# Two RWKV-style layers and an attention block: features turned inside weight blocks, preparation without GpSimd's arithmetic and barrier, recurrence calls joined through the next call's keys

## What is computed

```python
p = h @ w_in                       # gates, u, v of the SGU, and p_b
p_b = p + mu * (prev - p)          # token shift, on R, K, V and the LoRA columns
y_a = gelu(u) * (tril(w_s) @ layer_norm(gelu(v)) + b_s)
kk = normalised(k * k_k);  k = k * (1 + (a - 1) * k_a)
if layer: v = v + (v_first - v) * sigmoid(v0 + ...)
for t: sa = S @ kk_t
       S  = S * w_t - outer(sa, kk_t * a_t) + outer(v_t, k_t);  y_t = S @ r_t
y_b = group_norm(y) * gn_g + gn_b + sum(r * k * r_k) * v
x = x + (sigmoid(gate_a) * (y_a @ w_a) + sigmoid(gate_b) * (y_b @ w_b)) @ w_out
```

## Time and profile before

| | us |
|---|---|
| median of 3 runs | 2944.49 (2942.97 to 2948.69) |
| the profiled execution, its own time | 2934.4 |
| its span | 2932.6 |
| PE busy | 2667.9 (91%) |
| DVE busy | 1713.2 (58%) |
| ACT busy | 1396.8 (48%) |
| POOL busy | 117.2 (4%) |

### The profile page before, as it was taken

The page is one execution under the profiler, slowest core; times in us unless marked ns, Lnnn a source line. Parts: engine busy times, 40 slices in busy tenths (PEclk is TensorE's granted clock), DMA queues, the critical chain, the costliest instruction groups (busy, mean ns, idle before and its releaser), DMA issues.

```text
span 2932.6 us, 45086 instructions
## 1 busy us (share of the span) xinstructions
PE 2667.9 (91%) x17867; PEld 2146.8 (73%) x17867; DVE 1713.2 (58%) x1936; ACT 1396.8 (48%) x1677; POOL 117.2 (4%) x116
## 2 busy tenths in 40 slices
PE   6999888899999999688889999987999999998998
PEld 5877467677878876367777877855888887866786
DVE  4546635746545546734745555666777676555574
ACT  4434323534434434223535445365575674455573
POOL 0001100000000001300000000000000000011000
PEclk9999999999999999799999999998999999999899
DMA  5457812434454558522434553410445445432343
GB/s 192 179 187 253 329 60 81 170 132 172 172 201 158 197 186 291 209 89 70 176 133 171 200 184 146 189 56 29 182 178 188 171 172 199 173 114 89 141 185 116
DMA packets 73419, 477.79 MB, mean 163 GB/s; under 512 B 8830, under 2 KB 13020, under 8 KB 18864
## 3 DMA queue, kind: packets, MB, share of 16 engines
q1 hardware_dynamic: 60608, 440.43, 40.1%
q0 software_dynamic: 8048, 30.93, 3.0%
q10 hardware_dynamic: 4608, 4.20, 0.5%
HBM read 466.83 MB, written 2.13 MB: 160 GB/s over the span
## 4 chain that ended last, share of the span: by engine, by line
PE 73%; DVE 11%; DMA 5%; ACT 5%; issue 2%; DVEq 2%; POOL 0%; ACTq 0%; POOLq 0%; SPq 0%
PE ACC L428 63%; DMA raw<-wstream 4%; PE TP L428 4%; PE TP L504 3%; DVE w_lo L1496 3%; PE MM L428 2%; ACT w_hi L1018 2%; PE TP L690 1%; DVE ST L1994 1%; DMA BIAS<-toe 1%; DVE PR L2007 1%; DMA PREV<-V 1%; ACT XX L1152 1%; DVE ST L2082 0%; DMA COL<-cols 0%
## 5 line engine op out<-in xcount | busy, mean ns | idle before, releaser
L1496 DVE TENSOR_TENSOR w_lo<-raw,w_hi 128x2048 fp32r<-128x2048 f32 x371 | 841.9, 2289 | 438.1 <-ACT w_hi L1018 416.3
L1018 ACT ACTIVATE w_hi<-raw 128x2048 fp32r<-128x2048 f32 x371 | 703.4, 1916 | 434.3 <-DMA raw<-wstream 273.4
L428 PE MATMUL ACC<-w_hi,HA_hi 128*128 128x512 f32 (+1 forms) x2032 | 805.4, 396 | 32.0 <-DVE HA_lo L1573 13.8
L428 PE MATMUL ACC<-w_hi,HA_lo 128*128 128x512 f32 (+1 forms) x2032 | 795.0, 391 | 0.0
L428 PE MATMUL ACC<-w_lo,HA_hi 128*128 128x512 f32 (+1 forms) x2032 | 794.8, 391 | 0.0
L428 PEld LDWEIGHTS ACC<-w_hi,HA_hi 128*128 128x128 f32 x2032 | 387.0, 190 | 115.2 <-issue 25.5
L428 PEld LDWEIGHTS ACC<-w_hi,HA_lo 128*128 128x128 f32 x2032 | 386.5, 190 | 80.7
L428 PEld LDWEIGHTS ACC<-w_lo,HA_hi 128*128 128x128 f32 x2032 | 387.4, 191 | 76.5
L428 PE MATMUL ACC<-w_hi,FT_hi 128*128 128x512 f32 x616 | 246.0, 399 | 7.0 <-issue 7.0
L428 PE MATMUL ACC<-w_hi,FT_lo 128*128 128x512 f32 x616 | 244.2, 396 | 0.0
L428 PE MATMUL ACC<-w_lo,FT_hi 128*128 128x512 f32 x616 | 244.1, 396 | 0.0
(11 more groups left out here) (321 smaller groups left out, 3001.1 us busy)
## 6 DMA issues: line engine op xcount, KB each, us to landing
raw<-wstream SPq DMA_DIRECT2D x371, 1024.0 KB, 4.8
ADW<-wada SPq DMA_DIRECT2D x48, 1024.0 KB, 9.7
BC<-vecs POOLq DMA_DIRECT2D x16, 512.0 KB, 6.3
BIAS<-toe ACTq DMA_DIRECT2D x32, 128.0 KB, 2.8
BC<-mod_scr POOLq DMA_DIRECT2D x6, 512.0 KB, 4.3
WA<-lora POOLq DMA_DIRECT2D x2, 1024.0 KB, 14.5
PREV<-R POOLq DMA_DIRECT2D x4, 448.0 KB, 5.4
PREV<-K POOLq DMA_DIRECT2D x4, 448.0 KB, 5.7
```

Of the source, the lines that this page charges most:

```text
L428: return pe.matmul(*a, skip_group_check=True, **k)
L1018: act.activation(w_hi[:, s, :], unit, ACT.Copy).then_inc(sem["hi_ready"], 1)
L1496: dve.tensor_tensor(w_lo[:, s, :], unit, w_hi[:, s, :].bitcast(F32), ALU.subtract).then_inc(sem["lo_ready"], 1)
```

## The change

*Preparation.* BP's two products go from POOL to DVE, one ahead of T2, one behind AA; the r_k row is fetched before the seventh shift's transfers. The value residual goes to DVE: first half at the end of `prepare`, second half at the start of call 1. The exponential scaling of the second token half goes behind the first transposes: KK before the sum BN, the rest after the clearing of S. Modulation group 0 is summed inside call 0, in another bank (`SUM_BANK`). The barrier goes; PE waits for `keys_ready`.

*Recurrence.* ABT is doubled. The keys p = 0 and 1 of the next call are turned in the chain of this one, after the U product of each chunk, and copied by ACT after U. The next call starts at `s_done` with p = 2 and 3; `y_done` is awaited later. Of a call's four modulation units, 2, 2, 3 and 4 (by call) stay between the grams; one goes behind the first turn of XX in calls 0 to 2, and one in the chain ahead of the second chunk in calls 0 and 1.

*Gating.* The features of R are turned in the middle of the fifth and sixth block, those of VA in the middle of the two w_b blocks. ACT and DVE take features, evacuations and splits in a matching order.

```diff
         CC_IN, CC = ar("CC_IN", 93, [P, 2 * KT]), ar("CC", 93.5, [P, 2 * KT])
-        ABT = ar("ABT", 64, [P, 4, 4, P])
...
-    mod_sums(l, 0)
-    phase()
     for g in range(2):
         for t in range(NT):
             wkv_parallel(l, g, t)
-            wkv_chain(g, t)
+            wkv_chain(l, g, t)
     phase()
...
-    for j in range(6):
+    for j in range(4):
         block_wide(HA_hi, HA_lo)
-    features(R, "r_done")
+    block_wide(HA_hi, HA_lo, between=lambda: half_features(R, "r_done", 0))
+    block_wide(HA_hi, HA_lo, between=lambda: half_features(R, None, 1))
+    block_wide(HA_hi, HA_lo)
...
-    for j in range(2):
-        block_wide(HA_hi, HA_lo)
+    block_wide(HA_hi, HA_lo)
     need_features()
-    block_wide(HB_hi, HB_lo)
-    features(VA, "xn_ready")
-    block_wide(HB_hi, HB_lo)
+    block_wide(HB_hi, HB_lo, between=lambda: half_features(VA, "xn_ready", 0))
+    block_wide(HB_hi, HB_lo, between=lambda: half_features(VA, None, 1))
...
+def turned_keys(i, p):
+    g, t = divmod(i, 2)
+    for n, src in enumerate((KK, R, AA, K)):
+        last = pe.transpose(TP[1 - p % 2][:, P * n:P * n + P],
+                            src[:, t, P * (4 * g + p):P * (4 * g + p) + P], ident())
+    last.then_inc(sem["turned_ready"], 1)
+
 def wkv_parallel(l, g, t):
 
-    for p in range(4):
-        if p >= 2:
-            pe.wait_ge(sem["abt_ready"], c.next("abt_ready"))
-        for n, src in enumerate((KK, R, AA, K)):
-            last = pe.transpose(TP[p % 2][:, P * n:P * n + P],
-                                src[:, t, P * (4 * g + p):P * (4 * g + p) + P], ident())
-        last.then_inc(sem["turned_ready"], 1)
+    i = 2 * g + t
+    ABT = ABTS[i % 2]
+    in_grams, behind_turn = ((2, 1), (2, 1), (3, 1), (4, 0))[i]
+    if i == 0:
+        pe.wait_ge(sem["keys_ready"], c.next("keys_ready"))
+        pe.wait_ge(sem["ada_copied"], 3 * l + 1)
+        turned_keys(i, 0)
+        turned_keys(i, 1)
+    else:
+        pe.wait_ge(sem["s_done"], c.next("s_done"))
+    for p in (2, 3):
+        pe.wait_ge(sem["abt_ready"], c.next("abt_ready"))
+        turned_keys(i, p)
...
         if pair == 0:
-            at = 8 + 4 * (2 * g + t)
-            mod_units(l, at, at + 4)
+            if i == 0:
+                pe.wait_ge(sem["exp_ready"], c.next("exp_ready", 6))
+            unit = 8 + 4 * i
+            mod_units(l, unit, unit + in_grams)
+            if i == 0:
+                mod_sums(l, 0)
...
     for h in range(2):
+        if h:
+            mod_units(l, unit + in_grams, unit + in_grams + behind_turn)
         pe.wait_ge(sem["xt_ready"], c.next("xt_ready"))
...
-    if l and (g, t) == (0, 0):
+    if l and (g, t) == (0, 1):
         pe.wait_ge(sem["v_ready"], c.next("v_ready"))
+    if i:
+        pe.wait_ge(sem["y_done"], c.next("y_done", 2))
...
     for ch, rows in enumerate(CHUNKS):
         if t == 0 and ch == 0:
             pe.wait_ge(sem["s_zero"], c.next("s_zero"))
         if ch:
+            if i < 2:
+                mod_units(l, 11 + 4 * i, 12 + 4 * i)
             pe.wait_ge(sem["s_done"], c.next("s_done"))
...
+        if ch and i < 3:
+            pe.wait_ge(sem["abt_ready"], c.next("abt_ready", 0) + 1)
...
         last.then_inc(sem["uu_ready"], 1)
+        if i < 3:
+            if (i, ch) == (0, 0):
+                pe.wait_ge(sem["keys_ready"], c.next("keys_ready"))
+            turned_keys(i + 1, ch)
         pe.wait_ge(sem["u_copied"], c.next("u_copied"))
...
-    pe.wait_ge(sem["y_done"], c.next("y_done", 2))
-    pe.wait_ge(sem["s_done"], c.next("s_done"))
+    if i == 3:
+        pe.wait_ge(sem["y_done"], c.next("y_done", 2))
+        pe.wait_ge(sem["s_done"], c.next("s_done"))
...
+def turned(n, p):
+    act.wait_ge(sem["turned_ready"], c.next("turned_ready"))
+    act.activation(ABTS[n % 2][:, p, :, :].rearrange("p a n -> p (a n)"), TP[1 - p % 2][:, :], ACT.Copy) \
+        .then_inc(sem["abt_ready"], 1)
+
+def wkv(l, n, between=None):
+
+    if between:
+        turned(n, 0)
+        turned(n, 1)
+        between()
+    turned(n, 2)
+    turned(n, 3)
+    if n >= 2:
+        mod_copy(l, n - 1)
...
+    for ch, rows in enumerate(CHUNKS):
         act.wait_ge(sem["pp_ready"], c.next("pp_ready"))
         act.activation(PM[rows, 0, :, :], four(M[0][rows, 0:256]), ACT.Copy).then_inc(sem["pm_even"], 1)
         act.wait_ge(sem["uu_ready"], c.next("uu_ready"))
         act.activation(U[rows, :, :, :].rearrange("p a n x -> p a (n x)"), MM[rows, :, 256:512], ACT.Copy) \
             .then_inc(sem["u_copied"], 1)
+        if n < 3:
+            turned(n + 1, ch)
...
+        act.drain().then_inc(e.acc_free(), 1)
+
+    factors(1.0)
+    factors(1.0, -1.0)
+    factors(1.0)
     act.wait_ge(sem["gam_ready"], c.next("gam_ready"))
     act.activation(GAM[:, :], M[0][:, 0:32], ACT.Exp)
     mod_copy(l, 0)
-    phase()
-    for n in range(4):
-        wkv(l, n)
+    wkv(l, 0, between=lambda: factors(1.0, -1.0))
+    for i in range(1, 4):
+        wkv(l, i)
...
+    features_plain(HB_hi, (0,))
+    act.wait_ge(sem["gn_done"], c.next("gn_done"))
+    evacuate(cols(GATE_B, 0), "gate_ready", ACT.Sigmoid)
     squares(VA, SQ)
-    act.wait_ge(sem["gn_done"], c.next("gn_done"))
-    for j in range(2):
-        evacuate(cols(GATE_B, j), "gate_ready", ACT.Sigmoid)
-    features_plain(HB_hi)
+    features_plain(HB_hi, (1,))
+    evacuate(cols(GATE_B, 1), "gate_ready", ACT.Sigmoid)
+    evacuate(cols(UA, 0), "gelu_ready", ACT.Gelu_apprx_tanh)
     e.b += 2
     c.next("acc_ready", 2)
-    for j in range(2):
-        evacuate(cols(UA, j), "gelu_ready", ACT.Gelu_apprx_tanh)
+    evacuate(cols(UA, 1), "gelu_ready", ACT.Gelu_apprx_tanh)
+    features_plain(HA_hi, (0,))
     e.skip(2, 1)
     split(2)
-    features_plain(HA_hi)
...
-    v = vector()
+    ka, rk = vector(), vector()
+    tt(BP[:, :, :], R[:, :, :], both(rk), ALU.mult)
     dve.wait_ge(sem["asig_ready"], c.next("asig_ready", 2))
-    stt(T2[:, :, :], AA[:, :, :], -1.0, both(v), ALU.add, ALU.mult)
-    dve.drain().then_inc(sem["bc_free"], 1)
-    stt(whole(K), whole(T2), 1.0, whole(K), ALU.add, ALU.mult).then_inc(sem["k_ready"], 1)
+    stt(T2[:, :, :], AA[:, :, :], -1.0, both(ka), ALU.add, ALU.mult)
+    dve.drain().then_inc(sem["bc_free"], 2)
+    stt(whole(K), whole(T2), 1.0, whole(K), ALU.add, ALU.mult)
     dve.wait_ge(sem["rs_ready"], c.next("rs_ready"))
     tt(heads(KK), heads(KK), per_head(RS[:, :], 32, HD), ALU.mult)
     dve.drain()
     tt(whole(AA), whole(AA), whole(KK), ALU.mult)
     dve.drain()
+    tt(whole(BP), whole(BP), whole(K), ALU.mult)
     shift_mix(l, 6)
...
+    if l:
+        dve.wait_ge(sem["vf_land"], c.next("vf_land", 16))
+        dve.wait_ge(sem["vsig_ready"], c.next("vsig_ready", 2))
+        v_residual(0)
+    scaled_keys(0)
+    scaled_rest(0)
+    dve.drain().then_inc(sem["keys_ready"], 1)
...
+def v_residual(t):
+
+    tt(VF[:, t, :], VF[:, t, :], V[:, t, :], ALU.subtract)
...
+def wkv(l, g, t):
+
+    if (g, t) == (0, 1):
+        mod_columns(l, 0)
+        if l:
+            v_residual(1)
+            dve.drain().then_inc(sem["v_ready"], 1)
     if (g, t) == (0, 0):
+        scaled_keys(1)
         dve.tensor_reduce(BN[:, :, :].rearrange("p t h -> p (t h)"), heads(BP), AX.X, ALU.add)
     if t == 0:
         dve.drain()
         dve.memset(S[:, :, :], 0.0)
         dve.drain().then_inc(sem["s_zero"], 1)
+    if (g, t) == (0, 0):
+        scaled_rest(1)
+        dve.drain().then_inc(sem["keys_ready"], 1)
...
-    mod_columns(l, 0)
-    phase()
...
     pass_block()
     pass_block()
+    features_plain(HB_hi, HB_lo, (0,))
     dve.wait_ge(sem["gelu_ready"], c.next("gelu_ready", 2))
...
+    pass_block()
     dve.wait_ge(sem["ss_ready"], c.next("ss_ready"))
     rates(2, D, LN_EPS)
-    pass_block()
+    features_plain(HB_hi, HB_lo, (1,))
     v = vector()
...
-    features_plain(HB_hi, HB_lo)
+    e.skip(2, 1)
...
-    pass_block()
-    pass_block()
+    split(2)
     dve.wait_ge(sem["gelu_ready"], c.next("gelu_ready", 2))
     tt(whole(VA), whole(SQ), whole(UA), ALU.mult)
     dve.drain().then_inc(sem["xn_ready"], 1)
+    pass_block()
+    features_plain(HA_hi, HA_lo, (0,))
...
-            features_plain(HA_hi, HA_lo)
+            features_plain(HA_hi, HA_lo, (1,))
...
+        if n == 6:
+            vector(row(10 * l + V_RK))
         pool.wait_ge(sem["p_ready"], c.next("p_ready"))
...
     shifts(l)
-    s, landed = vector(row(10 * l + V_RK))
     if l:
         pool.wait_ge(sem["lo_ready"], PB_END[l])
         pool.dma_start(VF[:, :, :], vfirst_scr).then_inc(sem["vf_land"], 16)
-    pool.wait_ge(sem["mix_done"], 7 * l + 5)
-    pool.wait_ge(sem[f"bc{s}"], landed)
-    pool.tensor_tensor(BP[:, :, :], R[:, :, :], BC[:, s, :].unsqueeze(1).broadcast_to([P, NT, D]), ALU.mult) \
-        .then_inc(sem["bc_free"], 1)
-    pool.drain()
-    pool.wait_ge(sem["k_ready"], c.next("k_ready"))
-    pool.tensor_tensor(whole(BP), whole(BP), whole(K), ALU.mult).then_inc(sem["bp_ready"], 1)
```

(11 more changed lines are left out.)

93 lines of the change are left out of this document (41 added, 52 removed).

## The result

| us | before | changed |
|---|---|---|
| median | 2943.73 (2940.7 to 2948.69, 4 runs) | 2843.41 (2837.52 to 2848.39, 4 runs) |
| the profiled execution, its own time | 2934.4 | 2845.9 |
| forecast | | 2855.5 (2842 to 2890) |

The ratio is 0.965, with an interval of 0.962 to 0.968. The sign and the likeliest case were right. The gain was not: forecast 89.0, measured 100 to 103. Against the 2944.49 of the forecast the ratio gives 2841.4, just under the range's lower end. The two profiled executions differ by 88.5, almost the forecast number, and that is a coincidence. Between these two the six stages of the mixers are 98.2 shorter, and 9.7 are lost again outside them: T2 of layer 0 starts 3.1 later, and the last attention takes 7.9 longer.

What follows compares the result with a forecast made beforehand. PE bounds the kernel, busy 2667.9 of 2932.6 us, with gains where the mixers leave it waiting. Preparation -9.4 and -19.8, recurrence -8.4 and -6.5, gating -22.8 and -22.1 sum to -89.0: 2944.5 to 2855.5 us, range 2842 to 2890.

Steps and rivals of the forecast that it cites:

- the likeliest case: Whole kernel: all three parts pay, 89.0 us off the median, giving 2855.5 us; chance 0.70.
- Preparation: Ahead of the recurrence: stretched DVE products shrink once POOL's arithmetic goes; -9.4 us in layer 0, -19.8 in layer 1.
- The late r_k row: Preparation, layer 0: the row for BP's first product lands late, so T2 comes 0.8 to 4.3 us late; 1.5 taken.
- Recurrence: Chain of calls: keys turned early and modulation units moved; -8.4 us in layer 0, -6.5 in layer 1.
- I take -2.5, since the row is at the lower level: Join, from a call's last state to the next first LG: 2.5 us saved each, with transposes at 1.2 GHz.
- The value set aside, -3.3: Same joins at 2.4 GHz: 3.3 us saved each, put at 4.8 us better over six joins.
- The small terms: Recurrence: moved units gain 1.8 and 0.9; chain unit costs 0.4, chunk transposes 0.2 each; layer 1's residual join gains 0.2.
- Gating: PE's waits for a TP bank (20.0, 19.3 us) and their half-clock spells go: -22.8 and -22.1 us by layer.
- Half the gating's wait stayed: Rival, gating: one of two TP-bank waits per layer stays with its spell, 24 us in all, 2880; chance 0.15.
- Clock low in the chains: Rival, recurrence: one more 1.84 us half-clock spell per chunk pair and call, 15 us, 2870; chance 0.07.
- Weights late: Rival, gating's weight loads: units split in calls 2 and 3 come too late and stop the recurrence, 2945 and more; chance 0.03.
- More than the sum, below 2842: Rival: 2.4 GHz holds in chains and joins (4.8 us, first cause), and the weights' spells go as well; chance 0.05.

Runs made afterwards that it cites:

- the further chip: Three profiled executions of the unedited kernel before ran there: 2950.6, 2952.8 and 2965.2 us; one more run of before there took 2953.4.
- the kernel without the join: Changed kernel, but the next call's keys are turned at the start of their own call, after the last output copies: 2860.18 us, 16.1 above the changed kernel.

## Why the prediction fell short

- **Preparation, right.** Forecast 29.2, measured 28.7, less 0.4 for T2. All stretched products went back to 2.29 and 1.22. The late r_k row was a real cost, and about the size given to it: T2 of layer 0 started 0.3 to 2.1 us behind ACT's AA in the four executions, 1.1 on average, where it was 0.1 in before and with BP on POOL. One sign failed. The first transpose of layer 0 came at 332.1 to 334.0, not at 329.9, because PE was still on modulation units when the keys were ready (329.1 to 331.2). It cost little, since DVE was late for the grams anyway.
- **Recurrence, wrong in size: the term that failed.** "I take -2.5, since the row is at the lower level": a join gains 3.43 to 3.72, five times, and 0.29 in layer 1's call 1. Eight transposes take 1.0, not 1.7, because the granted clock is 1.00 there. The value set aside, -3.3, was nearer. (The prediction prices it at 4.8 over six joins; by its own working only five can gain, which is 4.0.) That is 5 of the 10 us missing. The other 5 were in no term of the sum, and they are not pinned down one by one. Part of them are second chunks at half clock, 5.7 to 6.0 us long instead of 4.4 or, with a unit, 4.8. The execution that I read had two, 5.94 and 5.75, and the sum left them as they were. In the five executions of before there are 15 among 40 second chunks, in the four of the changed kernel 3 among 32. Another part is that one execution was read, whose recurrences lie 2.3 and 2.7 below the mean of five, or 0.2 and 2.6 without the further chip. The Trainium skill's page "TensorE: Matmul & The Clock Gate", Part 4, says that transposes don't count as busy for the clock gate; by that rule the joins would have stayed at 0.50. They ran at 1.00 with and without a unit in the chain, so here the measurement decides against what I drew from it. These transposes are float32; no run here has others.
- The small terms held: 1.7 and 0.85 for units that left the grams (forecast 1.8 and 0.9), 0.35 a call for the unit in the chain (0.4), 0.1 for the transposes in a chunk (0.2), 0.29 for layer 1's join behind the residual (0.2). Layer 1's second LG of call 1, forecast 2.2 sooner, came 1.1 to 2.0 sooner. One term was missed: from its second LG to its first state, call 0 of layer 0 grew by 1.9 between the first two profiles (26.07 to 28.00) and by 1.2 on average (26.6 to 27.8). The units between the grams aren't the cause, for with them there it took 27.81. What goes with it is a fall of the granted clock some 9 us behind the second LG, in all four executions of the changed kernel (27.67 to 28.01), in one of five of before (27.67), and not in the kernel without the join (26.48). Changed, then before, at the same place; why it falls there stays open:

```profile
352.00:358.00 6.00, 5.27 (x119) 5.13 (x120) 1.27 (x3) 1.19 (x2) 0.00 (x0) 0.72 0.18 74
```

```profile
358.40:364.40 6.00, 5.55 (x182) 5.27 (x178) 1.69 (x4) 2.19 (x4) 0.00 (x0) 1.00 0.03 7
```

- **Gating, 4 us short.** The waits went as forecast. What stands behind them is 4.8 and 4.7 us a layer (24.8 - 20.0, 24.0 - 19.3), 2.3 to 2.4 for each wait instead of 1.65, and the 0.5 for the SGU product wasn't paid: the one wait of 2.4 that is left stands in both kernels.
- **Level, and range.** The sum was made against the fastest of five executions. Setting it on the median was right in itself, but the range's lower end, 2842, allowed 7 us for sizes and nothing for spells that the first profile happened not to have.
- **Rivals.** Half the gating's wait stayed: no, 0.3. Clock low in the chains: no. Weights late: no wait for one in calls 2 and 3. "More than the sum, below 2842" had 0.05; by the ratio it is what happened (2841.4), by the medians nearly (2843.4), and by its first cause.

## What to carry to other kernels

A wait of the matmul engine costs twice, once itself and once as half clock behind it, so that removing it gives more than its own length. Here the gating's stages gave 2.3 to 2.4 us beyond each wait, and putting one wait back cost 2.6 and 1.6. Before taking a row's low clock over into the time after a change, ask whether the clock is low only because of the wait that goes. And before summing small terms from one profiled execution, profile several: executions of one kernel differed by 12 us in one attention that nobody edited, and by 5 in a recurrence.

## What was not expected of the hardware

- A POOL product of 128x2048 takes 4.51 us when no product of DVE is under way at its start, and 6.51 when it starts while DVE is on one; the exclusion goes both ways. DVE's sum over a tile ran beside it at its usual 2.29.
- The granted clock at a join depends on little. With eight transposes in the chain and a wait of 0.56 us it was 1.00 at every join; with 0.89 more of waiting it was 1.00 at four and fell at one. With that wait and no transposes in the chain it held at one of six.
- Unedited code at the second layer's attention took 313.6 to 326.0 us in five executions of one kernel, and 319 to 326 in four of the other. The length follows the time at half clock, 27 us in the shortest and 58 in the longest. Why that time differs between executions stays open.
